# Expert layer of the latent tokens: every expert from tables read in order, with one-hot weight matrices, in place of gathered rows

## The reference, cut to what matters

```
qry   = (xb @ w_query).reshape(P, 8, 2, 128)
s     = einsum('phcd,hckd->phck', qry, sub_keys)          # 8 heads, 2 halves, 128 keys
top_s, top_i = top_k(s, 16)                               # 16 best of each half
cand_s = top_s[..., 0, :, None] + top_s[..., 1, None, :]  # 16 x 16 pairs a head
best_s, pos = top_k(cand_s, 16); idx = cand_i at pos      # 16 of 16384 experts a head
gate  = softmax(best_s)
act   = gelu(einsum('pd,phkd->phk', xb, u_tab[idx]))
out   = einsum('phk,phkd->pd', gate * act, v_tab[idx])
```

## Time and profile before

| what | value |
|---|---|
| median of three runs | 5276.8 us |
| profiled execution: its own time, its span | 5276.41 us, 5274.7 us |
| mean granted TensorE clock | 0.934 |
| TensorE busy in the span | 4244.9 us (80%) |
| VectorE busy in the span | 2888.3 us (55%) |
| data moved | 1037.05 MB, of it 805.36 MB by the gathers' queue |
| `q0n` and `q0`, four tiles | 2699.18 to 4247.93 us |
| `q1n` and `q1`, two tiles | 4463.66 to 5263.42 us |

### The profile page before, as it was taken

One profiled execution on the slowest core, in us unless ns is written; L12 is line 12 of the kernel. 1 busy time (PEld: TensorE's weight loads), 2 busy tenths in 40 slices (PEclk: granted clock), 3 DMA queues, 4 the chain that ended last, 5 costly groups with the idle time before them and its releaser, 6 DMA issues.

```text
span 5274.7 us, 45722 instructions
## 1 busy us (share of the span) xinstructions
PE 4244.9 (80%) x15314; PEld 2302.6 (44%) x15314; DVE 2888.3 (55%) x5960; ACT 846.3 (16%) x1852; POOL 1227.2 (23%) x1173
## 2 busy tenths in 40 slices
PE   7988789899978888887888777777687766677877
PEld 3333334754468787774574222222222224522222
DVE  3343321424546666663135887877876633688665
ACT  2231220006411111111011001001010022100001
POOL 0000000001034443340001333343343300133433
PEclk9988899999989898898999999999999988899999
DMA  4433242440010000002113989999999941398998
GB/s 178 152 112 128 112 161 95 184 152 34 32 40 1 1 1 1 1 1 80 64 57 153 398 342 407 388 354 399 352 387 422 421 166 40 123 397 332 420 421 357
DMA packets 128923, 1037.05 MB, mean 197 GB/s; under 512 B 14256, under 2 KB 14640, under 8 KB 16304
## 3 DMA queue, kind: packets, MB, share of 16 engines
q0 software_dynamic: 110592, 805.36, 38.1%
q1 hardware_dynamic: 18096, 228.77, 11.6%
HBM read 1030.93 MB, written 3.15 MB: 196 GB/s over the span
## 4 chain that ended last, share of the span: by engine, by line
PE 46%; DVE 29%; issue 8%; DMA 7%; POOL 5%; ACT 5%; DVEq 0%; POOLq 0%; SPq 0%; ACTq 0%
PE bank L192 27%; DVE arena L2484 9%; DMA arena<-in_uv,arena 6%; PE bank L1887 4%; POOL arena L2463 4%; ACT arena L204 4%; DVE arena L2489 3%; PE bank L2441 3%; DVE arena L210 3%; PE bank L1898 2%; PE bank L1500 1%; DVE arena L214 1%; ACT L204 1%; POOL arena L1980 1%; PE bank L1908 1%
## 5 line engine op out<-in xcount | busy, mean ns | idle before, releaser
L2441 PE MATMUL bank<-arena 128*128 128x512 f32 x3072 | 1550.8, 631 | 494.8 <-DVE arena L2489 494.5
L192 PE MATMUL bank<-arena 128*128 128x512 f32 (+4 forms) x5408 | 1625.9, 459 | 112.8 <-ACT arena L204 48.7
L192 PEld LDWEIGHTS bank<-arena 128*128 128x128 f32 (+1 forms) x5408 | 861.1, 182 | 828.1 <-issue 670.0
L2441 PEld LDWEIGHTS bank<-arena 128*128 128x128 f32 x3072 | 535.6, 193 | 1506.7 <-DVE arena L2489 1078.5
L2463 POOL DMA_INDIRECT arena<-in_uv,arena x768 | 808.4, 1053 | 1466.6 <-PE bank L2441 884.5
L2484 DVE CUSTOM_DVE_ANT_0 arena<-arena 128x1024 f32<-128x1024 f32 x768 | 942.4, 1227 | 278.4 <-DMA arena<-in_uv,arena 212.4
L204 ACT ACTIVATE arena<-arena 128x1 f32<-128x1 f32 (+7 forms) x1070 | 309.5, 289 | 2863.0 <-DVE arena L2484 1852.8
L204 ACT ACTIVATE arena<-bank 128x512 f32<-128x512 f32 (+4 forms) x512 | 283.4, 554 | 1393.6 <-PE bank L192 646.5
L2489 DVE TENSOR_SCALAR arena<-arena 128x128 f32<-128x128 f32 x768 | 292.5, 381 | 285.1 <-ACT arena L204 267.0
L1980 POOL TENSOR_TENSOR arena<-arena 128x512 f32<-128x512 f32 x224 | 285.7, 1276 | 448.6 <-PE bank L1887 356.3
L1887 PE MATMUL bank<-arena 128*128 128x128 f32 x1792 | 281.0, 313 | 65.2 <-POOL arena L1980 65.2
(11 more groups left out here) (238 smaller groups left out, 2504.8 us busy)
## 6 DMA issues: line engine op xcount, KB each, us to landing
arena<-in_ada_w SPq DMA_DIRECT2D x24, 2048.0 KB, 8.1
arena<-in_w_in SPq DMA_DIRECT2D x16, 2048.0 KB, 8.0
arena<-in_w_mod SPq DMA_DIRECT2D x12, 2048.0 KB, 8.2
arena<-in_dn_w SPq DMA_DIRECT2D x12, 2048.0 KB, 8.2
arena<-in_w_up SPq DMA_DIRECT2D x11, 2048.0 KB, 8.1
arena<-in_wq SPq DMA_DIRECT2D x8, 2048.0 KB, 8.1
arena<-in_uv,arena POOLq DMA_INDIRECT x768, 9.8
arena<-in_w_down SPq DMA_DIRECT2D x5, 2048.0 KB, 7.2
```

The source lines that it names most:

```text
L192: t = p.e.matmul(out, l, r, start=(i == 0), stop=(i == n - 1))
L2441: t = p.e.matmul(by[half], m["dg"][ee % 4], m["uv"][r][:, 1024 + 512 * half:1536 + 512 * half], start=(ee == 0), stop=(ee == 127))
```

## The change

Stage `q0` keeps `peer` with gathers, but for tiles 0 and 1 alone. For tiles 2 and 3 new stages `e0` (after `q0`) and `e1` (in place of `q1`) run a dense form:

- `pe_dense` makes the queries for 256 tokens, the scores of tile 2, then goes through the whole `u` table: 64 chunks of 1 MB (256 experts), each 16 matmuls of 256 columns, with a Gelu over 512 columns by ScalarE into `act`, an array of 16384 experts x 256 tokens that takes 128 KB of each partition, ring included.
- VectorE selects tile 2 during these chunks (`dve_choose`). Its `dve_weights` waits for an exponential that ScalarE issues after the 64 Gelus. Then, for each tile, in 16 groups of 8 tokens: VectorE compares an index row with 0 to 127 to make one-hot matrices A and B (two operations over 1024 elements), GpSimd multiplies A by the gates, TensorE makes for each token a 128 x 128 weight matrix (8 matmuls of 128 columns), and VectorE multiplies `act` by it in place, 4 tokens an operation. `dve_choose` of tile 3 stands between the groups of tile 2 and those of tile 3.
- After the last group TensorE goes through the `v` table: 64 chunks of 1 MB, each 8 matmuls of 512 columns, into four PSUM banks.
- The 1 MB chunks go through three buffers of their own, loaded by SyncE. The context rows of x serve as scratch, so they are stored to and reloaded from `xrest` around `e0`.

The core of the diff, in this order: `sp_dense`, `pe_dense`, `dve_dense`, `pool_dense`, `layout`, `sp_program`, `act_program`.

```
+        for n in range(128):
+            if n > 2:
+                s.wait_ge(*(P.of(k + ".u", n - 3) if n < 67 else P.of(k + ".v", n - 67)))
+            s.e.dma_start(m["ring"][n % 3], self.I["ut"][l][n] if n < 64 else self.I["v"][l][:, n - 64, :]
...
+        for c in range(4):
+            ch = self.ring.use(p, 8, 512)
+            run(self.pe_channels(p, f"{k}.q{c}", ch, hL, range(4), slice(0, 256), lambda j: A.of(k + ".q", c, j)))
...
+        scores(0)
+        for n in range(64):
+            if n == self.SECOND:
+                scores(1)
+            p.wait_ge(*self.loaded(m, n))
...
+            for j in range(2):
+                t = mm(p, b[:, 256 * j:256 * j + 256], [(ch[:, j, d, :], hL[:, d, :]) for d in range(8)])
...
+        for n in range(2):
+            p.wait_ge(*V.of(k + ".gate", n))
...
+            for g in range(16 * n, 16 * n + 16):
+                A_, B_ = m["hot"][g % 2]
+                p.wait_ge(*V.of(k + ".B", g))
+                p.wait_ge(*G.of(k + ".A", g))
+                for u in range(2):
+                    b = self.banks.take(p, k + ".G", g, u)
+                    for q in range(4):
+                        t = p.e.matmul(b[:, H4[q]], A_[:, 4 * u + q, :], B_[:, 4 * u + q, :], start=True, stop=True)
...
+        p.wait_ge(*V.of(k + ".G", 31, 1))
+        for n in range(64):
+            p.wait_ge(*self.loaded(m, 64 + n))
...
+            for j in range(2):
+                for i in range(2):
+                    for half in range(2):
+                        t = p.e.matmul(by[i][half], act_[:, 2 * n + j, H4[i]], ch[:, j, 512 * half:512 * half + 512],
...
+        def hot(g):
...
+            v.wait_ge(*(P.of(k + ".G", g - 2, 1) if g > 1 else P.of(k + ".u", 63)))
+            v().tensor_tensor(A_, bc(m["iota128"], 1, 8), bc(T[:, 0, s], 2, 128), ALU.is_equal).then_inc(*V.up(k + ".A", g))
+            v().tensor_tensor(B_, bc(m["iota128"], 1, 8), bc(T[:, 1, s], 2, 128), ALU.is_equal).then_inc(*V.up(k + ".B", g))
...
+        def weigh(g):
+            for u in range(2):
+                w = m["act"][:, :, 8 * g + 4 * u:8 * g + 4 * u + 4].rearrange("p j t -> p t j")
...
+                v().tensor_tensor(w, w, heads(self.banks.at(k + ".G", g, u), 4), ALU.mult).then_inc(*V.up(k + ".G", g, u))
...
+            for g in range(16 * n, 16 * n + 16):
+                hot(g)
+                if g:
+                    weigh(g - 1)
+        for n in range(2):
+            run(self.dve_choose(v, m, k, n, P.of(k + ".ijT", 0) if n else None))
+            self.dve_weights(v, m, k, n, m["gate"])
+            gates(n)
...
+            g_.wait_ge(*V.of(k + ".A", g))
+            A_ = m["hot"][g % 2][0]
+            g_().tensor_tensor(A_, A_, bc(m["ijgT"][n][:, 2, s], 2, 128), ALU.mult).then_inc(*G.up(k + ".A", g))
...
-        L["q0"] = self.mem_peer(0, [0, 1, 2, 3])
+        L["q0"] = self.mem_peer(0, [0, 1])
+        L["e0n"] = norm([2, 3])
+        L["e0"] = self.mem_dense(0)
...
+        self.all_done(s, "q0")
+        s.e.dma_start(self.xrest[:, 0:2048], xflat[:, 0:2048]).then_inc(*D.up("xc.out", 0))
+        self.sp_dense(s, L["e0"], "e0")
+        self.all_done(s, "e0")
+        s.wait_ge(*D.of("xc.out", 0))
+        s.e.dma_start(xflat[:, 0:2048], self.xrest[:, 0:2048]).then_inc(*D.up("xc.in", 0))
...
+        a.wait_ge(*D.of("xc.in", 0))
         self.act_norm(a, "a2n", L["a2n"], x, [0, 1, 2, 3])
```

More of the change, by code:

```diff
@@ L2266, in mem_peer @@
         nt = len(tiles)
-        r = dict(nt=nt, t0=tiles[0], layer=layer, qry=self.a3(16, 128 * nt), keys=self.a3(16, 128))
+        r = dict(nt=nt, t0=tiles[0], layer=layer, sides=sorted({i // 2 for i in tiles}), qry=self.a3(16, 128 * nt), keys=self.a3(16, 128))
         r["g2"] = [self.alloc(1024) for _ in range(2)]
@@ L2468, in dve_peer @@
         P, V, A, t0, nt, M = self.P, self.V, self.A, m["t0"], m["nt"], self.M[1 + m["layer"]]
[L2469 to L2473, removed]
+        for s in m["sides"]:
+            if s != m["sides"][0]:
+                v.wait_ge(*P.of(f"{k}0.bc", 1))
+            self.dve_bcast(v, f"{k}{s}", M[:, 40:48, 1 - s], m["wide"])
         run(self.dve_select(v, m, k, 0))
@@ L2495, in dve_peer @@
             v.wait_ge(*P.of(k + ".y", n, 127))
-            for s in range(2):
-                if s == 1 or t0 == 0:
-                    v.wait_ge(*A.of(f"{k}{s}.row", 1))
+            for s in m["sides"]:
+                v.wait_ge(*A.of(f"{k}{s}.row", 1))
             for half in range(2):
@@ new lines, in act_dense, with scores, late @@
+    def act_dense(self, a, m, k):
+        P, V, A, l = self.P, self.V, self.A, m["layer"]
+        def scores(n):
+            for c in range(4):
+                a.wait_ge(*P.of(k + ".s", n, c))
+                if n == 0 and l == 0:
+                    a.wait_ge(*self.D.of("xc.out", 0))
+                if n:
+                    a.wait_ge(*V.of(k + ".ij", n - 1))
+                act(a, m["s"][:, 512 * c:512 * c + 512], self.banks.at(k + ".s", n, c), ACT.Copy
+                    ).then_inc(*A.up(k + ".s", n, c))
+        def late(n):
+            self.act_exp(a, m, k, n)
+            a.wait_ge(*P.of(k + ".ijT", n))
+            act(a, m["ijgT"][n], self.banks.at(k + ".ijT", n)[:, 0:384].rearrange("p (c t) -> p c t", c=3), ACT.Copy
+                ).then_inc(*A.up(k + ".ijT", n))
+        for c in range(4):
+            for j in range(4):
+                a.wait_ge(*P.of(f"{k}.q{c}", j))
+                act(a, m["qry"][:, 4 * c + j, :], self.banks.at(f"{k}.q{c}", j)[:, 0:256], ACT.Copy
+                    ).then_inc(*A.up(k + ".q", c, j))
+        scores(0)
+        for n in range(64):
+            if n == self.SECOND:
+                scores(1)
+            if n == 52:
+                for c in range(2):
+                    a.wait_ge(*P.of(k + ".s", c, 3))
+            a.wait_ge(*P.of(k + ".u", n))
+            act(a, m["act"][:, 2 * n:2 * n + 2, :], self.banks.at(k + ".u", n).rearrange("p (j t) -> p j t", j=2), ACT.Gelu
+                ).then_inc(*A.up(k + ".act", n))
+        for n in range(2):
+            late(n)
+        self.act_bcast(a, k, m["g2"])
@@ L2787, in layout @@
         self.top = self.base
-        L["q1n"] = norm([2, 3])
-        L["q1"] = self.mem_peer(1, [2, 3])
+        L["e1n"] = norm([2, 3])
+        L["e1"] = self.mem_dense(1)
         L["fi"] = self.mem_final()
@@ L2841, in sp_program @@
             return
-        self.sp_peer(s, L["q1"])
-        for _ in range(3):
-            ring.skip()
+        self.sp_dense(s, L["e1"], "e1")
         if self.stop < 7:
```

208 lines of the change are left out of this document (169 added, 39 removed).

## The result

The kernel after takes 6179.7 us (median of four runs, 6173.57 to 6180.24), the kernel before on the same chip 5275.3 us: a ratio of 1.1709, with a 95% interval of 1.1689 to 1.1729. That is 904 us slower. The forecast was 6156 us, slower, with 6240 as the upper end. The profiled execution took 6173.57 us with a span of 6171.9 us, 17.6 us over the predicted 6154.3.

What follows compares the result with a forecast made beforehand. Gather loops were held bound by DMA, gapless stretches by TensorE. Span 5274.7 - 1548.8 (latent-token stages removed) + 2 x (12.8 + 1197.9) (dense stages) + 7 (reload) = 6154.3 us; predicted 6156, forecast range 6085 to 6185 (50%), upper end 6240.

Steps and rivals of the forecast that it cites:

- the two-tile stage: `q1n` with `q1` before the change, 799.8 us, taken as the time of the new `q0n` and `q0`.
- turn: Between u table and groups, VectorE waits for the exponential behind Gelu 63: 5 us, allowing 3 to 8.
- second selection: Tile 3's `dve_choose` behind tile 2's groups, with no dense work to cover it: 71.1 us, all exposed.
- reload: At the end `a2n` waits for the context rows to be loaded again: 7 us.
- The groups: 16 each for tiles 2 and 3, at 4.4 us: 140.8 us, plus 2.6 at the end.
- The rival that paid for the steps: Weighting pays for its 1 KB steps: 4.98 us a group, 37 us more, 6193 us in all; chance 25%.
- The tables: Dense u and v streams at TensorE's float32 pace: 453.3 us with tile 3's scores, and 456.8 us; streams 900.5 a layer.
- the lower bound: Lower end of the range: groups at 3.94 us (-29), streams at 6.91 us a chunk (-31), and the turn.
- The tail: Behind the v table's matmuls, four operations of 0.73 us: 3 us.
- The tables limited by transfers: Rival: DMA, not TensorE, limits the streams, 2.57 us a chunk, 329 us a layer, 5014 us in all; chance 2%.
- Slow v loads: Rival: 8 KB pieces 512 KB apart in HBM load slowly, 10.3 us a chunk, 6578 us in all; chance 4%.
- VectorE and GpSimd hindering each other: Rival: GpSimd's product can't run beside A and B, groups 5.04 to 6.49 us, 6197 to 6290 us; chance 12%.

Runs made afterwards that it cites:

- the last run: Gathers kept except last layer's dense form (bfloat16, early selections, tokens-first `act`); tokens and weighted activations rounded, not cut off, against the same kernel truncated: 5091.0 us, ratio 0.9659.

## Why the prediction was right, point by point

**Direction and size** were right for the reason given: 256 gathered choices at the DMA rate against two whole tables at TensorE's pace. Half of the matmuls took away 881 us, so the tables in float32 cost what their matmuls cost; in bfloat16 the same loads take 372 us a layer, less than the 674 of the gathers. The direction hung on one number, the pace of a float32 matmul read from the earlier trace rows.

**Terms that were right within 2 us a layer**: the two-tile stage, norm, queries, turn, second selection, weights, broadcast, reload. Most had a row of the same work in the kernel before; the turn, the broadcast and the reload were put together from smaller rows or taken by estimate. `q0` was taken whole from the two-tile stage and came 1.1 us off.

**The groups** were mis-sized, 143.4 predicted, 169.7 measured, 26 us a layer. By the prediction's own sign ("I am wrong if ... the groups take over 5 us") this part of it was wrong: in the steady state a group takes 5.25. The step is "I take 4.4, by the row of the contiguous operation": the weighting's elements lie 1 KB apart, and no row showed such an operation. It takes 1260 ns instead of 688, the contiguous version gives 4.3 us a group, and leaving GpSimd's product out leaves the weighting at 1260. The rival that paid for the steps, with 4.98 and a chance of 25%, was the true mechanism and its size was a little low: it took 0.52 us more for each weighting, measured are 0.57, and with the small gaps between VectorE's operations a group is 5.25. By the Trainium skill ("SBUF — State Buffer", the note on cachelines) each crossing to another line pays a penalty; the two runs agree with a price for the step, 1260 against 688 ns, and say nothing of the size of a line.

**The tables** were over-sized. The u table was taken at 0.2196 us a record and runs at 0.2166; the v table at 0.440 and runs at 0.430. The 3 us for the slow clock at its start did not come: the window of its first 10 us shows 0.96. With the streams at 6.91 us a chunk as the lower bound had them, 6.93 and 6.88 were measured. That is 19 us a layer less. The slow clock was in fact counted twice. Both rows from which the paces were read begin with it: 0.74 in the first 10 us of the up projection, 0.83 from 1102 to 1112 us in the down projection of the kernel before. At 0.2166 and 0.430 us a record the two stretches would be 2.1 and 1.8 us shorter than they are, which is about what those windows lose (2.6 and 1.7). The row with 512 records at 0.216 us, whose first window shows 0.97, was the better one.

**The tail** was counted as four operations; there are eight, of 0.73 us each (two for each quarter, an addition from PSUM and one from SBUF). That is 2.8 us a layer more, a miscount in reading the change.

**The total** fits better than its terms: +26 and +3 against -19 and -2 a layer leave 8 to 10 us a layer, 17.6 in all. That the total came within 18 us is partly luck: a miss of 26 us and one of 19 us a layer, of opposite sign and unrelated cause.

**The rivals.** The tables limited by transfers: no, for float32, as half of the matmuls with all of the loads showed, at 430 ns a record and two records a matmul; the 131 ns for a matmul of 512 columns that the Trainium skill gives ("TensorE: Matmul & The Clock Gate", back-to-back issue gap) is not seen in any run here; in bfloat16 it is 0.25 us. Slow v loads: no, they land in 4.8 us as the contiguous u loads in 4.7. VectorE and GpSimd hindering each other: only in one A a layer, 3 us in all. But GpSimd's product takes 2.93 us, not 2.55, and in the shorter groups of the contiguous run it is felt: there TensorE waits 1.63 us for it (at 4056.77).

**Where the difference between the forms lies.** Of 1220 us a layer, 884 are tables, 71 the exposed selection, 170 the groups. Both selections under the table and the contiguous weighting take 131 / 2 + 61 / 2 = 96 us a layer off, worked out from the single runs; together they ran only with bfloat16. Some 1120 us would be left in float32, against 799.8 with gathers, and of them 884 are the two tables alone. So at this pace of a float32 matmul no order of the rest reaches the gathers. A dense form in full float32 with fewer columns wasn't tried.

## What to carry to other kernels

Before a gather is replaced by a pass over the whole table, price the table twice, by the bytes at the DMA rate and by the columns at TensorE's pace for that data type; the larger one was the time here, and in float32 it was TensorE's by more than a factor of two (6.9 against 3.0 us a chunk). Where an array must be strided for one engine, give the stride to the one that has idle time in that stage, and read that from the windows. An exponential in the middle of a stream of another function belongs a chunk or two ahead of the point at which its result is wanted, else the engines behind it stand for the table load, as TensorE did here for 3.25 us.

## What the runs showed of the hardware

The same 1 MB load lands in 4.7 to 4.8 us when a chunk is asked for every 6.9 us, in 4.9 and 4.7 when every 3.45, and in 6.8 to 6.9 with three always under way; the rate then is 352 GB/s, below the 408 of the indirect gathers of 8 KB rows.

A step of 1 KB costs VectorE 1260 instead of 688 ns for 512 elements, a step of 512 bytes costs ScalarE's write 1.03 to 1.06 instead of 0.60 us, and one of 512 bytes 294 instead of 189 ns in a weight load of TensorE.

The stretch ahead of the change, the same in all kernels, is not equally long in all of them. In the chain of waits the 512 records of one stage begin at these times, first for the run with two buffers, then for the last run:

```profile
2599.75 110.93 PE bank L192 x512
```

```profile
2584.55 110.93 PE bank L192 x512
```

Before has 2587.59. So the start of the changed part moves by up to 15 us for reasons that the edit doesn't show, and whose cause stays open. A difference as small as the 3 us of GpSimd's product is therefore read from the stages and not from the whole.
